# Layer 1's expert sums: part of V read densely, seven U buffers, one-hot weights multiplied on GpSimd

## The reference, cut to what matters

```python
q = (x @ w_q).reshape(t, 8, 2, 128)
scores = einsum('thcd,cnd->thcn', q, sub_keys)
top_s, top_i = top_k(scores, 16)
cand_s = top_s[..., 0, :, None] + top_s[..., 1, None, :]
cand_i = top_i[..., 0, :, None] * 128 + top_i[..., 1, None, :]
...
best_s, pos = top_k(cand_s, 16)
idx, g = take(cand_i, pos), softmax(best_s)
...
a = gelu(einsum('tkd,td->tk', u[idx], x)) * g
out = einsum('tk,tkd->td', a, v[idx])
```

## Time and profile before

| what | value |
|---|---|
| time, median of 3 runs | 3602.56 us (3600.56 to 3604.57) |
| the profiled execution's own time | 3597.09 us |
| its span in the profile | 3595.0 us |
| mean granted TensorE clock | 0.913 |
| moved by DMA | 1345.35 MB, 374 GB/s over the span |
| close of window 0, 1, 2, 3 (start of line 1987) | 1146.7, 2047.1, 2947.3, 3589.0 us |

### The profile page before, as it was taken

How to read it: one execution, slowest core, us unless ns; L and a number is a source line. 1 busy time by engine, 2 the same in 40 slices (tenths; PEclk the granted TensorE clock), 3 DMA queues, 4 the chain that set the end, 5 groups by cost and what they waited for, 6 DMA issues and landing times.

```text
span 3595.0 us, 26702 instructions
## 1 busy us (share of the span) xinstructions
PE 2877.5 (80%) x7322; PEld 1355.1 (38%) x7322; DVE 2034.9 (57%) x3584; ACT 945.4 (26%) x2349; POOL 1456.3 (41%) x1065
## 2 busy tenths in 40 slices
PE   7888977777786888888788788998988867776766
PEld 6445743333332433333333233443433322222222
DVE  2333156666667554555464655455546467677765
ACT  3334322222222223323221222332322122222221
POOL 4002545555655322222343532322234355555554
PEclk8877988898998999999998899999999988888888
DMA  4212599999999999999999999999999989999998
GB/s 144 82 61 89 195 386 416 416 412 415 418 419 421 418 417 417 417 417 413 409 406 400 408 418 417 417 417 417 413 412 410 400 362 421 421 421 421 422 420 360
DMA packets 262853, 1345.35 MB, mean 374 GB/s; under 512 B 27200, under 2 KB 48192, under 8 KB 130368
## 3 DMA queue, kind: packets, MB, share of 16 engines
q0 software_dynamic: 147456, 1073.81, 72.2%
q1 hardware_dynamic: 115264, 269.99, 19.9%
HBM read 1341.62 MB, written 2.10 MB: 374 GB/s over the span
## 4 chain that ended last, share of the span: by engine, by line
DMA 61%; PE 20%; issue 12%; POOL 3%; DVE 2%; ACT 1%; SPq 1%; DVEq 0%; POOLq 0%; ACTq 0%
DMA room<-in_peer_v_dram,index 51%; PE psum L981 11%; DMA wbuf<-in_fox_w_o_dram 5%; DMA wbuf<-in_peer_w_q_dram 4%; PE psum L1030 2%; PE psum L1045 2%; POOL room L672 1%; PE psum L744 1%; PE psum L745 1%; PE psum L746 1%; POOL room L682 1%; DMA room<-in_peer_u_dram,index 1%; DVE resid L1978 0%; SPq L539 0%; POOL w_low L656 0%
## 5 line engine op out<-in xcount | busy, mean ns | idle before, releaser
L981 PE MATMUL psum<-room,diag 128*128 128x512 f32 x3072 | 1605.6, 664 | 554.2 <-DMA room<-in_peer_v_dram,index 493.9
L1967 DVE CUSTOM_DVE_ANT_0 room<-room,normed 128x2048 f32<-128x2048 f32 x512 | 1172.8, 2291 | 613.7 <-DMA room<-in_peer_u_dram,index 609.4
L682 POOL DMA_INDIRECT room<-in_peer_v_dram,index x512 | 749.4, 1464 | 1083.3 <-PE psum L981 1050.1
L981 PEld LDWEIGHTS psum<-room,diag 128*128 128x128 f32 x3072 | 603.6, 208 | 1497.0 <-issue 1239.8
L672 POOL DMA_INDIRECT room<-in_peer_u_dram,index x512 | 590.7, 1154 | 729.5 <-DVE dots L1967 482.4
L1396 ACT ACTIVATE acts<-dots 128x1 f32<-128x1 f32 x512 | 103.4, 202 | 1765.6 <-DVE dots L1967 1765.2
L1978 DVE SCALAR_TENSOR_TENSOR resid<-room,acts,resid 128x512 f32<-128x512 f32 x512 | 384.2, 750 | 306.6 <-DMA room<-in_peer_v_dram,index 236.8
L1045 PE MATMUL psum<-wbuf,normedT 128*128 128x512 f32 x1024 | 463.6, 595 | 0.0
L1030 PE MATMUL psum<-wbuf,normedT 128*128 128x512 f32 x512 | 272.4, 682 | 83.4 <-DMA wbuf<-in_peer_w_q_dram 41.8
L1045 PEld LDWEIGHTS psum<-wbuf,normedT 128*128 128x128 f32 x1024 | 188.9, 190 | 214.7 <-issue 212.0
L656 POOL TENSOR_TENSOR w_low<-wbuf,w_high 128x2048 fp32r<-128x2048 f32 (+1 forms) x28 | 113.9, 4080 | 304.4 <-ACT w_high L1251 304.4
(11 more groups left out here) (199 smaller groups left out, 1800.8 us busy)
## 6 DMA issues: line engine op xcount, KB each, us to landing
wbuf<-in_fox_w_in_dram SPq DMA_DIRECT2D x128, 1024.0 KB, 12.5
wbuf<-in_fox_w_o_dram SPq DMA_DIRECT2D x32, 1024.0 KB, 31.9
wbuf<-in_peer_w_q_dram SPq DMA_DIRECT2D x32, 1024.0 KB, 28.2
wbuf<-in_mla_w_o_dram SPq DMA_DIRECT2D x16, 1024.0 KB, 5.1
wbuf<-in_peer_w_q_dram SPq DMA_DIRECT2D x32, 512.0 KB, 9.1
wbuf<-in_mla_w_in_dram SPq DMA_DIRECT2D x8, 1024.0 KB, 8.3
wbuf<-in_mla_w_kvb_dram SPq DMA_DIRECT2D x32, 256.0 KB, 3.4
room<-in_peer_u_dram,index POOLq DMA_INDIRECT x512, 16.6
```

The source lines that it names most:

```text
L682: pool.indirect_dma_start(v_ring[:, r, :], None, v_table, bass.IndirectOffsetOnAxis(index[:, number % 2, s:s + 1], 0)).then_inc(v_full[r], 16)
L981: mm = pe.matmul(psum[:, q, :], diag[:, r, :], v_ring[:, r, q * TILE:(q + 1) * TILE], start=at == 0, stop=at == WINDOW - 1, skip_group_che ...
L1967: V.tensor_tensor_reduce(u_ring[:, r, :], u_ring[:, r, :], normed[:, b, :], 1.0, 0.0, ALU.mult, ALU.add, dots[:, r:r + 1]).then_inc(dot_do ...
```

## The change

It concerns windows 2 and 3 and what comes behind them; windows 0 and 1 keep their code.

**U.** From slot 256 on, U tiles go into seven buffers (`deep`): the four of the U ring and three of the V ring's. `gather_deep(n)` waits for the dot of seven slots before. The fourth V buffer and `scores_ahead` hold tables: both keys, the row number and the activation of every slot and token of a block.

**V, columns 768 to 2047** (1280 columns, 5 KB a row) are still gathered, 128 tiles for each block (`gather_part`), into four buffers. None is gathered in window 2. In window 3 88 tiles of block 0 are gathered and summed by TensorE through diagonal matrices (`sum_part`, three products), spread over 124 slots by `v_at`. The other 40 of block 0 and all 128 of block 1 are added by VectorE (`add_part`, scalar times 1280 columns plus residual) behind window 3.

**V, columns 0 to 767** are read densely: `load_dense(i)`, i = 0 to 127, brings the 128 experts of first key i, 128 rows of 3 KB, into four buffers, and `dense(i)` multiplies them with `spread[b][:, i, :]` for both blocks (512 and 256 columns each, four products). `spread[b]` (128 second keys x 128 first keys x 128 tokens) holds every token's activations at its experts' places. It is made in 32 groups of 4 tokens for each block. For a group, VectorE compares both keys, turned so that choices lie on partitions, with 0 to 127 (`one_hots`, 1024 columns out); GpSimd multiplies the activations into one of the two one-hot matrices (`weigh`, 512 columns); TensorE makes four 128 x 128 products (`spread_tokens`); ScalarE copies 512 columns out (`copy_spread`). The one-hot buffers are two. Block 0's groups lie in window 3, one for every 3.5 slots from slot 8; block 1's come behind window 3. ScalarE no longer makes diagonal matrices in slots of windows 2 and 3.

```diff
+DENSE = 768
+KEPT = D - DENSE
+GATHERED = 2 * WINDOW
+SPLIT = 2 * WINDOW
+LAST = 3 * WINDOW
+DEEP = 7
+AHEAD = DEEP - RING
+ON_PE = 88
+TOKENS = 4
+BUILDS = P // TOKENS
+BUILD_AT = 8
+def v_at(m):
+    return 3 + m * 124 // ON_PE
+def build_at(g):
+    return BUILD_AT + g * 7 // 2
...
+            def load_dense(i):
+                r = i % RING
+                if i == 0:
+                    sp.wait_ge(dot_done, UNITS * SLOTS)
+                    sp.wait_ge(index_ready, UNITS)
+                if i >= RING:
+                    sp.wait_ge(tile_used, i - RING + 1)
+                sp.dma_start(v_tile[r], peer_v[1][i * KEYS:(i + 1) * KEYS, 0:DENSE]).then_inc(tile_full[r], 16)
...
+            def gather_deep(n):
+                number, s = n // SLOTS, n % SLOTS
+                m = n - SPLIT
+                r = m % DEEP
+                if s == 0:
+                    pool.wait_ge(index_ready, number + 1)
...
+                else:
+                    pool.wait_ge(dot_done, n - DEEP + 1)
...
+            def gather_part(m):
...
+                if RING <= m < ON_PE + RING:
+                    pool.wait_ge(part_summed, m - RING + 1)
+                if m >= ON_PE + RING:
+                    pool.wait_ge(part_added, m - RING - ON_PE + 1)
+                pool.indirect_dma_start(v_part[r], None, v_table,
+                                        bass.IndirectOffsetOnAxis(late_place[b][:, at:at + 1], 0),
+                                        element_offset=DENSE).then_inc(part_full[r], 16)
+            def weigh(b, g):
+                number = BUILDS * b + g
+                pool.wait_ge(hot_ready, number + 1)
+                tokens = slice(TOKENS * g, TOKENS * (g + 1))
+                pool.tensor_tensor(hot_act[g % 2], hot_act[g % 2],
+                                   turned[b][:, 2, tokens].unsqueeze(2).broadcast_to([P, TOKENS, KEYS]),
+                                   ALU.mult).then_inc(weighed, 1)
+            def last_window(at):
+                for m in range(ON_PE):
+                    if at == v_at(m) + AHEAD:
+                        gather_part(m)
+                for g in range(BUILDS):
+                    if at == build_at(g) + AHEAD:
+                        weigh(0, g)
...
+            for g in range(BUILDS):
+                weigh(1, g)
+                if g and g % 4 == 0:
+                    gather_part(ON_PE + RING - 1 + g // 4)
+            for m in range(ON_PE + RING + BUILDS // 4 - 1, GATHERED):
+                gather_part(m)
...
+            def spread_tokens(b, g):
+                number = BUILDS * b + g
+                bank = 6 + g % 2
+                pe.wait_ge(hot_ready, number + 1)
+                pe.wait_ge(weighed, number + 1)
+                if number > 1:
+                    pe.wait_ge(spread_done, number - 1)
+                for t in range(TOKENS):
+                    last = pe.matmul(psum[:, bank, t * P:(t + 1) * P], hot_key[g % 2][:, t, :], hot_act[g % 2][:, t, :],
+                                     start=True, stop=True)
+                last.then_inc(spread_full, 1)
+            def dense(i):
+                r = i % RING
+                pe.wait_ge(tile_full[r], 16 * (i // RING + 1))
+                if i == 0:
+                    pe.wait_ge(spread_done, NB * BUILDS)
+                    pe.wait_ge(sums_closed, 1)
+                for b in range(NB):
+                    for c0, n, bank in ((0, TILE, 3 + 2 * b), (TILE, DENSE - TILE, 4 - 2 * b)):
+                        mm = pe.matmul(psum[:, bank, 0:n], spread[b][:, i, :], v_tile[r][:, c0:c0 + n],
+                                       start=i == 0, stop=i == KEYS - 1, skip_group_check=True)
+                mm.then_inc(tile_used, 1)
...
+            def one_hots(b, g):
...
+                if number > 1:
+                    dve.wait_ge(spread_full, number - 1)
+                tokens = slice(TOKENS * g, TOKENS * (g + 1))
+                V.tensor_tensor(hots[g % 2], pick[:, :, :].unsqueeze(2).broadcast_to([P, 2, TOKENS, KEYS]),
+                                turned[b][:, 0:2, tokens].unsqueeze(3).broadcast_to([P, 2, TOKENS, KEYS]),
+                                ALU.is_equal).then_inc(hot_ready, 1)
...
+                close_parts()
+                for g in range(BUILDS):
+                    one_hots(1, g)
+                    if g % 4 == 3:
+                        add_part(ON_PE + g // 4)
+                for m in range(ON_PE + BUILDS // 4, GATHERED):
+                    add_part(m)
+                for b in range(NB):
+                    add_dense(b)
```

More of the change, by code:

```diff
@@ L1183, in job, with sum_part @@
                     pq_quarter(b, (at - PQ_AT) // 4, (at - PQ_AT) % 4)
+            def sum_part(m):
+                r = m % RING
+                if m == 0:
+                    pe.wait_ge(peer_added, 2)
+                pe.wait_ge(diag2_ready, m + 1)
+                pe.wait_ge(part_full[r], 16 * (m // RING + 1))
+                for c0 in range(0, KEPT, TILE):
+                    n = min(TILE, KEPT - c0)
+                    mm = pe.matmul(psum[:, c0 // TILE, 0:n], diag[:, r, :], v_part[r][:, c0:c0 + n],
+                                   start=m == 0, stop=m == ON_PE - 1, skip_group_check=True)
+                mm.then_inc(part_summed, 1)
@@ new lines, in turn_tables @@
+            def turn_tables(b):
+                pe.wait_ge(diag_ready, (3 + b) * WINDOW)
+                if b == 0:
+                    pe.wait_ge(score_done, 8)
+                else:
+                    pe.wait_ge(index_ready, UNITS)
+                for m in range(3):
+                    src = act_of[b] if m == 2 else keys_of[b][:, m, :]
+                    last = transpose(psum[:, 5, m * P:(m + 1) * P], src)
+                last.then_inc(turned_full, 1)
+            def spread_tokens(b, g):
[9 more added lines that the diff above has]
+                last.then_inc(spread_full, 1)
@@ L1185, in peer, with last_window @@
+            def last_window(at):
+                if at == 1:
+                    turn_tables(0)
+                for m in range(ON_PE):
+                    if at == v_at(m) + 3:
+                        sum_part(m)
+                for g in range(BUILDS):
+                    if at == build_at(g) + 1:
+                        spread_tokens(0, g)
             def peer():
@@ L1188, in peer @@
                     window, at = n // WINDOW, n % WINDOW
-                    accumulate(n)
+                    if window < 2:
+                        accumulate(n)
+                    if window == 3:
+                        last_window(at)
                     if window == 0 and at // SLOTS < PHEADS - 1:
@@ L1197, in peer @@
                         job(window - 1, at)
+                for at in range(WINDOW, WINDOW + 4):
+                    last_window(at)
+                turn_tables(1)
+                for g in range(BUILDS):
+                    spread_tokens(1, g)
+                for i in range(KEYS):
+                    dense(i)
             pe.wait_ge(consts_made, N_CONST)
@@ L1393, in slot @@
                 act.wait_ge(dot_done, n + 1)
-                if n >= RING:
+                if RING <= n < SPLIT:
                     act.wait_ge(axpy_done, n - RING + 1)
@@ L1614, in peer @@
                         job(window - 1, at)
+                    if window == 3:
+                        last_window(at)
+                for at in range(WINDOW, WINDOW + 4):
+                    last_window(at)
+                copy_tables(1)
+                for g in range(BUILDS):
+                    copy_spread(1, g)
             norm(0)
@@ L1990, in b_norm, with add_dense @@
+            def add_dense(b):
+                dve.wait_ge(tile_used, KEYS)
+                for c0, n, bank in ((0, TILE, 3 + 2 * b), (TILE, DENSE - TILE, 4 - 2 * b)):
+                    cols = resid[:, b, c0:c0 + n]
+                    last = V.tensor_tensor(cols, psum[:, bank, 0:n], cols, ALU.add)
+                    if c0 == 0:
+                        step(last)
+                chain.settle()
+                last.then_inc(dense_added, 1)
             def b_norm(b, ffn):
@@ L2115, in peer @@
                         job(window - 1, at)
-                axpy(UNITS * SLOTS - 1)
-                close(3)
+                    if window == 3:
+                        for g in range(BUILDS):
+                            if at == build_at(g):
+                                one_hots(0, g)
+                close_parts()
+                for g in range(BUILDS):
+                    one_hots(1, g)
[5 more added lines that the diff above has]
+                    add_dense(b)
             norm(0)
```

171 lines of the change are left out of this document (158 added, 13 removed).

## The result

The changed kernel takes 3667.42 us, the median of four runs (3663.53 to 3675.47). The kernel before, on the same chips, takes 3601.84 us (3600.56 to 3604.57). The ratio is 1.0186, with a 95% interval of 1.0170 to 1.0201: slower by 66 us. The prediction said 3655 us and slower, for GpSimd as the new bound.

A forecast was written before the change was run, and what follows sets the result against it. Transfers bound the kernel before; GpSimd was to bound window 3 after. Window 2, window 3, turn, groups, dense and end, 604 + 495 + 4 + 106 + 383 + 8 = 1600 us against 1547.9, gave 3655 us, range 3560 to 3712.

The forecast's parts named there:

- Window 2: Window 2 stays bound by DMA: 585 us of transfers plus 19 us for gaps, 604 us (590 to 650).
- The gaps: Two DMA gaps in window 2, from the attention job's chain and the last 14 slots: 19 us for both.
- Window 3: GpSimd, held by VectorE's work, becomes the bound of window 3: 495 us (450 to 540).
- The transfers' pace in window 3: Window 3's transfers alone, 121 U tiles and 88 tiles of 5 KB: 447 us.
- The lookahead: In window 3, U buffers only four ahead at a waiting product; this alone costs nothing.
- Turn and groups: Behind window 3, about 4 us of turn, then block 1's 32 one-hot groups in a serial chain, 106 us (62 to 134).
- The hole in the transfers: During block 1's groups, DMA near 2 tenths for some 100 us, idle for some 84 us.
- Dense tiles and parts: Behind the groups, the remaining transfers of 377 us set the pace: 383 us (377 to 430).
- The end: At the kernel's end, two pairs of additions and the store: 8 us.
- transfers as the bound in all stages: Rival for all changed stages: GpSimd keeps up, window 3 and groups under 549 us; 3558 us, chance 0.26.
- The short part ring: Rival for the last stage: four part buffers turn too slowly, 33 us on top; 3688 us, chance 0.12.
- Window 2 at 660 us: Rival: window 2 doesn't shorten as its transfers do, the job waiting across engines; 3711 us, chance 0.08.

The follow-up runs named there:

- b2: e7 with a part of V added with every one of block 1's groups; 3576.7 us, 0.9938 of before.
- e3: Changed kernel with window 3's dots covering 1024 of 2048 columns; 3617.1 us (one run).
- e1: Changed kernel with the product moved from GpSimd to VectorE, behind its comparison; 3606.2 us, 1.0019 of before.
- e7: Changed kernel with comparison and product in one operation on VectorE, so no products on GpSimd; 3598.8 us, 1.0001 of before.
- b1: e7 with a part of V added with every second of block 1's groups; 3588.0 us, 0.9972 of before.
- b3: b2 with the U gathers of window 2 only four ahead, seven again in window 3; 3563.21 us, 0.9904 of before.
- e4: Changed kernel with four U buffers in place of seven, which also left one tile ahead at a product; 3821.4 us, 1.0617 of before.
- c1: b2 with four U buffers in place of seven, no product on GpSimd; 3603.8 us.
- e6: Changed kernel with GpSimd filling the 512 columns with a constant in place of the product; 3614.0 us (one run).
- e2: Changed kernel with block 0's 32 products in window 3 left out, block 1's kept on GpSimd; 3634.6 us (one run).

## Why the prediction was right

The sign, the size and the reason held: GpSimd and VectorE exclude each other, GpSimd sets window 3, and block 1's groups stand bare in a hole. It named 1600 us for the stages; the profiled execution, 8 us above the median, has 1619.5. How near window 3 came is in part luck. Step by step:

- **Window 2**, 604 predicted, 612.3 measured; within 590 to 650. The gaps were sized rightly: packets take 96.7% of the stage, so DMA idles for 20 us of it, where 19 were put on both gaps. It does so almost wholly at the end, in pauses like those of b2 above. What was short are the transfers, 592 us of packets where 585 were priced.
- **Window 3**, 495 predicted, 509.6 measured. The total is right to 3%, though its terms are not, and that they cancel is luck. U gathers came to 1.93 us (1.35 predicted), part gathers to 1.56 (2.15), products to 1.58 (1.29 and a wait of 1 us). By these 128 x (1.93 + 0.3) + 88 x (1.56 + 0.3) + 32 x (1.58 + 0.5) = 516 us. The gathers of U came out 74 us over their term, those of parts 52 us under it. Scaling both kinds from their rows of before was the weak step: the extra belongs to whichever gather falls into a dot, and which one does is a matter of the order. Over both kinds a gather takes 1.77 us, and the prediction's mean was 1.68. That VectorE causes it, e3 shows; that 32 products tip the window over the transfers' pace, e1 shows.
- **The transfers' pace in window 3**, 447 predicted: 456 in e1, e3, e7, b1, b2 and b3, at a DMA share of 1.01.
- **The lookahead**, costed at nothing with four tiles ahead at a product: GpSimd's 10.6 us of waits for comparisons and e3 bear this out. With one tile ahead it costs some 121 us (e4 less c1's depth), and four buffers without products cost 42 us (c1).
- **Turn and groups**, 110 predicted, 97.1 measured, of which 5.3 are the turn and 92 the 32 groups: 2.87 us a group where 13.5 / 4 = 3.4 was worked out. The product takes 1.05 us undisturbed, not the 1.29 read off GpSimd's subtractions. The groups of the hole in the changed kernel:

```profile
L2297 DVE TENSOR_TENSOR normed<-pick,normed 128x1024 f32<-128x1024 f32 x32 | 55.5, 1736 | 20.9 <-PE psum L1367 20.8
...
L803 POOL TENSOR_TENSOR normed<-normed 128x512 f32<-128x512 f32 x32 | 44.2, 1382 | 30.3 <-DVE normed L2297 30.2
```

Alone the two operations take 1.22 and 1.05 us. Here they average 1.74 and 1.38 and add up to 99.7 us in 92 us of time: each blocked start is in its operation's record. The two engines take turns with nothing between, which is the serial chain that the prediction priced. With a fill in its place (e6) the hole is 25 us shorter.

- **The hole in the transfers**: "near 2 tenths" was said, 0.28 is the share.
- **Dense tiles and parts**, 383 predicted, 395.0 measured, within 377 to 430, but a step of it failed. A part does turn in 2.17 us when the ring is alone, within the 2.0 to 2.25 worked out. But the step that took 377 / 160 = 2.36 us a part for the whole stage spread the parts evenly over the stage, and the dense tiles do not wait for them: their stream ends 61 us early, and the last 28 parts take 61 us where their transfers take 45. b2 confirms it from the other side: with 23 parts fewer its two streams end nearly together.
- **The end**, 8 predicted, 5.6 measured.

The rivals: transfers as the bound in all stages (3558 us) is refuted by 509.6 + 97.1 = 607 us (601 without the turn), over the 549 set for it. Even with no product on GpSimd its stages come to 1550 us (e7), not the 1503 of its sum: window 2 takes 614 and not 596, the last stage 399 and not 377. The short part ring (3688) was half right: the ring costs time, but only behind the dense tiles, 16 us and not 33. Window 2 at 660 us did not come.

## What to carry to other kernels

Before work goes to GpSimd because it looks idle, look up whether it reads SBUF, and what two-input work VectorE does at that time. Here 32 products of 1 us each cost about 53 us in one window, and 32 more 16 us behind it, and a single VectorE operation that compares and multiplies at once made them needless. A gather issued by GpSimd counts at its length between VectorE's operations (here up to 3.1 us, not 0.94), so an engine at "40% busy" may have no room. Where two streams share the transfers, look at which ends first: behind it the other runs at its ring's pace, and moving some of its work to an earlier hole (b2) gave 22 us.

## What the runs showed of the hardware that was not expected

The length of a gather's issue on GpSimd follows VectorE's work, more than any other work of GpSimd's own. The mean over U and part gathers in window 3 is 1.77 us in the changed kernel, 1.75 without products (e1), 1.80 in e2 and 1.70 in b2, all with whole dots at 3.6 to 4.0 us a slot. It is 1.16 us at 3.6 us a slot with dots of half the length (e3), and in the kernel before, at 5.0 us a slot, it is 1.40 over U and V gathers. The kinds apart scatter more (U from 1.68 us in e6 to 1.96 in e1), so neither kind alone is a measure of how full VectorE is. A dot, by contrast, is not stretched by a gather's issue: 2.290 us in e6, with as many gathers as in the changed kernel. And GpSimd's product of 512 columns with an operand repeated along the columns took 1.05 us undisturbed, less than its subtractions into fp32r had made me expect (0.74 us for 256 columns, 4.61 for 2048).
